# Two heads of a pair issued alternately on the halves of the partitions, in score matmuls and index dots

## The chip, the core and the metric

One core of one Trainium2 chip runs the whole kernel in one launch. TensorE multiplies, VectorE and ScalarE work on the results, GpSimd (POOL) issues some DMAs and small powers, SyncE (SP) issues the loads of the weights. Each has a queue of its own, in program order, and they meet at semaphores. The metric is the device time in microseconds from launch to end. The median of three runs before the change is 2491.6 us.

## What is computed

Two transformer blocks over 256 tokens of width 2048, all in float32. The first block (an attention layer and a retention layer) is not touched. The second has two kinds of attention over 16 heads each, of width 64:

```python
dots = jnp.einsum('bqhd,bsd->bqhs', qi, k_idx).astype(jnp.float32)
index_score = jnp.einsum('bqh,bqhs->bqs', wi.astype(jnp.float32),
                         jax.nn.relu(dots)) * IDX_SCALE
...
_, sel = lax.top_k(index_score, topk)
...
s = jnp.where((dist >= 0)[:, :, None, :], s + bias, NEG_INF)
p = jax.nn.softmax(s, axis=-1).astype(c_sel.dtype)
o_lat = jnp.einsum('bqhk,bqkr->bqhr', p, c_sel)
```

The 16 index heads (width 64) give a score for each pair of query and key, and the 64 best keys of each query are kept. The sliding-window attention (heads of groups 0 and 1 below) has a bias, a window and a sink; the selected attention (groups 2 and 3) has a bias and the selection. Behind both come an output projection and a gated feed-forward layer with a convolution.

## The kernel before

The weights pass in blocks of 16 x 128 rows by 512 columns, each in four chunks. SP loads chunk c of a block into `raw`, ScalarE rounds it to `w_hi` (`round_hi`), VectorE takes the rest, `w_lo` (`split_lo`), and TensorE multiplies: 24 matmuls of 512 columns a chunk (`project`, `output`, with `product`, L364 to L371). `raw`, `w_hi` and `w_lo` have one place per chunk, so the load of chunk c of the next block waits until TensorE is through with chunk c of this one. ScalarE and VectorE run three chunks ahead: `act_blocks` and `vec_blocks` make chunk 3 of this block in slot 0 and chunks 0 to 2 of the next block in slots 1 to 3.

Between the chunks each engine does the attention work that is written for that slot. Its order is fixed by hand, in three lists: `B_STEPS` for TensorE, `B_ACT_STEPS` for ScalarE, and the table in `before` of `vec_second_attention` for VectorE. TensorE's slot c comes behind chunk c. ScalarE's and VectorE's slot c comes ahead of the rounding or the rest of chunk c - 1 of the next block.

Four groups g of eight heads h pass in this way, one during each of the blocks `B_B0 + 5` to `B_B0 + 8`. A head is these steps:

- TensorE, a score step (`s`): two matmuls of keys and queries over 64 partitions. Tokens 0 to 127 see 128 keys, tokens 128 to 255 see 256. Even heads lie in partitions 0 to 63, odd heads in 64 to 127 (`half`), and they write the PSUM banks `sc[0]` and `sc[1]`. The step of head n waits until VectorE has read head n - 2 from its bank (`b_read`).
- VectorE, `head(h)`: adds the bias into `b_s` (this is the read, L2093), in groups 2 and 3 also the selection (L2096), and takes the maxima (L2099; L2103 in groups 0 and 1).
- ScalarE, `s`: two exponentials with their sums (L1829).
- TensorE, `t`: three transposes into `turn` (L1473). ScalarE, `t`: a copy to `b_pT` (L1815).
- TensorE, `v`: three value products into `pair[1]` (L1483 to L1485).

VectorE also looks for the largest index scores in rounds (`topk`) in slots of groups 0 and 1. In group 3, and behind it, it adds each chunk of the output projection to the residual (`vec_scaled_sum`), and TensorE's next chunk waits for the first half of that (`b_scaled`).

The index dots (L1549) come before this, in the block `B_B0 + 3`: after chunks 1, 2 and 3 TensorE does the heads of `INDEX_HEADS`. Each is two matmuls, into `sc[h % 2]`; ScalarE takes the relu (L1767), and VectorE adds it, weighted, to `b_idx` (L2018), one head after the other.

Of the kernel before, what the change touches and what calls it, by code (L numbers as in the profile page):

```python
# [25 lines left out]
P = 128  # L26
D = 2048
T = 256
# [16 lines left out]
COPIES = 32  # L45
VEC_A, VEC_R, VEC_F = 45, 37, 16

INDEX_HEADS = {1: range(0, 4), 2: range(4, 9), 3: range(9, 16)}

A_B0 = 0  # L50
R_B0 = A_B0 + 4 * A_KV
# [64 lines left out]
def build(nc, x, attn_w_in, attn_q_gain, attn_k_gain, attn_w_out, ret_w_in, ret_decay_exp,  # L116
# [5 lines left out]
    with ctx:  # L122
# [90 lines left out]
        b_kBT = take("b_kBT", [8, T])  # L213
# [1096 lines left out]
        def pool_first_block(g):  # L1310
# [113 lines left out]
            with g.Fori(1, R_HEADS - 1) as i:  # L1424
# [5 lines left out]

        B_STEPS = {1: ["s0", "s1", "s2"], 2: ["t0", "s3", "t1", "s4", "v0"],
                   3: ["s5", "t2", "v1", "s6", "t3", "v2", "s7", "t4", "v3", "t5", "v4", "t6", "v5", "t7",
                       "v6", "v7"]}
        B_ACT_STEPS = {1: ["s0", "s1", "s2"], 2: ["t0", "s3", "t1", "s4"],
                       3: ["t2", "s5", "t3", "s6", "t4", "s7", "t5", "t6", "t7"]}
        HALF = W_HD

        def half(h):  # L1440
# [12 lines left out]
        def pe_b_step(pe, g, what):  # L1453
            kind, h = what[0], int(what[1])
            n = 8 * g + h
            if kind == "s":
                pe.wait_ge(sem("b_qT_b"), g + 1)
                pe.wait_ge(sem("b_qT_a"), g + 1)
                if n >= 2:
                    pe.wait_ge(sem("b_read"), n - 1)  # L1460
                keys = (lambda w: b_kaT[half(h), g, 0:w]) if g < 2 else \
                       (lambda w: b_kBT[half(h), 4 * (g - 2) + h // 2, 0:w])
                mm = three(sc[h % 2], lambda to, t, w: pe.matmul(
                    to, b_qT[half(h), h // 2, t * P:(t + 1) * P], keys(w), start=True, stop=True))
                mm.then_inc(sem("b_score"), 1)
            elif kind == "t":
                pe.wait_ge(sem("b_prob"), n + 1)
                if h < 2 and g > 0:
                    pe.wait_ge(sem("b_ol"), 4 if g == 3 else 2 * g)
                if n >= 2:  # L1470
                    pe.wait_ge(sem("b_pT"), n - 1)
                for m in range(3):
                    mm = pe.transpose(turn[h % 2][:, m * P:(m + 1) * P], b_s[:, h % 4, m * P:(m + 1) * P],  # L1473
                                      ident[:, :])
                mm.then_inc(sem("b_p_turned"), 1)
            else:
                pe.wait_ge(sem("b_pT"), n + 1)
                if h == 0 and g > 0:
                    pe.wait_ge(sem("b_og"), g)
                val = (lambda k: b_va[:, k, g * HALF:(g + 1) * HALF]) if g < 2 else \  # L1480
                      (lambda k: b_vB[:, k, (8 * (g - 2) + h) * HALF:(8 * (g - 2) + h + 1) * HALF])
                col = slice(h * HALF, (h + 1) * HALF)
                pe.matmul(pair[1][0][:, col], b_pT[:, h % 2, 0:P], val(0), start=True, stop=True)  # L1483
                pe.matmul(pair[1][1][:, col], b_pT[:, h % 2, P:2 * P], val(0), start=True, stop=False)
                pe.matmul(pair[1][1][:, col], b_pT[:, h % 2, 2 * P:3 * P], val(1), start=False, stop=True)\  # L1485
                    .then_inc(sem("b_pv"), 1)
# [17 lines left out]
        def pe_second_attention(pe):  # L1504
# [31 lines left out]
            def index(c):  # L1536
                if c == 0:
                    pe.wait_ge(sem("i_kdup"), 1)
                    pe.wait_ge(sem("gate_row"), 8)
                    pe_transposes(pe, sc[0], i_kdup, [0]).then_inc(sem("i_k_turned"), 1)  # L1540
                    return
                if c == 1:
                    pe.wait_ge(sem("i_kT"), 1)
                    pe.wait_ge(sem("i_qT_a"), 2)
                    pe.wait_ge(sem("i_qT_v"), 2)
                for h in INDEX_HEADS[c]:
                    if h >= 2:
                        pe.wait_ge(sem("i_relu"), h - 1)
                    three(sc[h % 2], lambda to, t, w: pe.matmul(  # L1549
                        to, i_qT[half(h), h // 2, t * P:(t + 1) * P], i_kT[half(h), 0:w],  # L1550
                        start=True, stop=True)).then_inc(sem("i_dot"), 1)
            project(pe, B_B0 + 3, pair[1], after=index)

# [409 lines left out]
        def vec_second_attention(v):  # L1964
# [110 lines left out]
            for g in range(4):  # L2075
                def start(g=g):
                    if g == 0:
                        v.wait_ge(sem("sink_in"), 16)
                        vec(v.tensor_scalar(b_nsink[:, :], b_sink[:, :], -1.0, None, ALU.mult))
                        topk(2)  # L2080

                def head(h, g=g):

                    n = 8 * g + h
                    if h == 0:
                        v.wait_ge(sem("bias_in"), 16 * 2 * (P // COPIES) * (g + 1))
                        if g == 2:
                            v.wait_ge(sem("sel"), 1)
                    v.wait_ge(sem("b_score"), n + 1)
                    if n >= 4:  # L2090
                        v.wait_ge(sem("b_p_turned"), n - 3)
                    s = b_s[:, h % 4, :]
                    v.tensor_tensor(s, sc[h % 2][:, 0:384], b_bias[:, h, :], ALU.add).then_inc(sem("b_read"), 1)  # L2093
                    v.wait_ge(sem("b_read"), n + 1)
                    if g >= 2:
                        vec(v.tensor_tensor(s, s, b_sel[:, :], ALU.add))  # L2096
                        vec_wait(v)
                    for t, w in ((0, slice(0, P)), (1, slice(P, 384))):
                        ins = v.tensor_reduce(b_nm[:, h, t:t + 1], s[:, w], AX, ALU.max, negate=True)  # L2099
                    if g < 2:  # L2100
                        vec(ins)
                        vec_wait(v)
                        ins = v.tensor_scalar(b_nm[:, h, :], b_nm[:, h, :], b_nsink[:, 8 * g + h:8 * g + h + 1],  # L2103
                                              None, ALU.min)
                    ins.then_inc(sem("b_max"), 1)

                def steps(c, g=g):
                    if g == 0 and c in (1, 2):
                        topk(1)
                    if g == 1 and c == 1:  # L2110
                        topk(1)
                        select()
                def finish(g):

                    if g < 2:
                        v.wait_ge(sem("b_max"), 8 * g + 8)
                        v.tensor_tensor(b_es[:, :, :], b_nm[:, :, :],
                                        b_sink[:, 8 * g:8 * g + 8].unsqueeze(2).to_broadcast([P, 8, NT]),
                                        ALU.add).then_inc(sem("b_esx"), 1)
                        v.wait_ge(sem("b_es"), g + 1)  # L2120
                        vec(v.tensor_tensor(b_ri[:, :, :], b_sum[:, :, :], b_es[:, :, :], ALU.add))
                        vec_wait(v)
                        vec(v.reciprocal(b_ri[:, :, :], b_ri[:, :, :]))
                    else:
                        v.wait_ge(sem("b_prob"), 8 * g + 8)
                        vec(v.reciprocal(b_ri[:, :, :], b_sum[:, :, :]))
                    vec_wait(v)
                    v.wait_ge(sem("b_pv"), 8 * g + 8)
                    if 1 <= g <= 2:
                        v.wait_ge(sem("b_o_turned"), 2 * g)  # L2130
                    if g == 3:
                        v.wait_ge(sem("b_q_turned"), 8)
                    for t in range(NT):
                        ins = v.tensor_tensor(gview(b_out(g)[:, t, :], 8), gview(pair[1][t][:, :], 8),
                                              b_ri[:, :, t].unsqueeze(2).to_broadcast([P, 8, HALF]), ALU.mult)
                    ins.then_inc(sem("b_og"), 1)

                def before(c, g=g):

                    if g == 3:  # L2140
                        vec_scaled_sum(v, "b_scaled", c, CH * (B_B0 + 8) + c + 1, c, pair[0], b_tmp, 0)
                    for h in {1: (0, 1, 2), 2: (3, 4), 3: (5, 6, 7)}.get(c, ()):
                        head(h)
                        if h == 0 and 1 <= g <= 2:
                            vec_b_outT(v, g - 1)
                    if c == 3:
                        finish(g)
                vec_blocks(v, B_B0 + 5 + g, {0: [start], **{c: [lambda c=c, s=steps: s(c)] for c in (1, 2, 3)}}, before)
# [215 lines left out]
```

## Time and profile before

| | |
|---|---|
| time, median of three runs | 2491.6 us (2485.77 to 2497.4) |
| profiled execution, span from the first to the last instruction | 2493.1 us |
| own time of that execution outside the span | not listed; it can't be told which of the three it is |
| granted TensorE clock, mean | 0.957 |
| TensorE (PE) busy | 2324.4 us (93%) |
| weight loads (PEld) busy | 1914.7 us (77%) |
| VectorE (DVE) busy | 1737.8 us (70%) |
| ScalarE (ACT) busy | 962.3 us (39%) |
| index stage (first to last dot) | about 1385 to 1409 us of the span |
| four groups of eight heads | about 1448 to 1638 us of the span |

Busy times overlap. A matmul's record is longer than its share of the stream, since matmuls are pipelined: two records that follow each other overlap by their ends, and the distance from start to start is what a matmul costs. The granted clock is a share of full speed: 1.00 is 2.4 GHz and 0.50 is 1.2 GHz.

### The profile page before, as it was taken

Reading aid. Unit: us, or ns where it says so; the run is one execution under the profiler, and the core shown is the slowest. Engines: PE = TensorE matmul, PEld = TensorE weight load, DVE = VectorE, ACT = ScalarE, POOL = GpSimd, SP = SyncE. Lnnn points to the kernel's source line nnn. Section 1 sums busy time; section 2 is a strip of 40 time slices with the busy share of each in tenths; the row PEclk is TensorE's granted clock in tenths of the full one; section 3 lists DMA queues with packets and bytes.
Section 4 is the critical chain, followed back from the end, with each engine's and each line's share of the span. In section 5 each row is a group of like instructions: output and inputs, shape, how many; then the busy total and the mean of one; then the engine's idle time right before and its main releaser. Section 6 shows DMA issues by size and latency. Waiting matters only on the chain.

```text
span 2493.1 us, 29352 instructions
## 1 busy us (share of the span) xinstructions
PE 2324.4 (93%) x10764; PEld 1914.7 (77%) x10764; DVE 1737.8 (70%) x2035; ACT 962.3 (39%) x987; POOL 178.4 (7%) x194
## 2 busy tenths in 40 slices
PE   6899998779999999999879999998999999999996
PEld 5778887657888888888668777777788888888885
DVE  6787876987877778778773554677466666666666
ACT  3433433333333333333323343434444444444442
POOL 4110000320000000000010000000000000000000
PEclk8999999889999999999988988989999999999998
DMA  6786775458778677787543444334555555555552
GB/s 220 263 267 228 254 257 192 161 202 296 250 245 294 234 261 272 242 274 263 201 137 112 133 123 123 115 119 152 183 188 185 185 185 186 187 188 189 193 185 101
DMA packets 261801, 501.29 MB, mean 201 GB/s; under 512 B 16753, under 2 KB 70289, under 8 KB 261104
## 3 DMA queue, kind: packets, MB, share of 16 engines
q1 hardware_dynamic: 230656, 382.39, 46.5%
q0 software_dynamic: 30512, 114.93, 13.6%
q10 hardware_dynamic: 576, 3.21, 0.3%
q8 instruction: 36, 0.59, 0.1%
q14 instruction: 21, 0.17, 0.0%
HBM read 496.80 MB, written 3.67 MB: 201 GB/s over the span
## 4 chain that ended last, share of the span: by engine, by line
PE 47%; issue 36%; DVE 10%; DMA 4%; ACT 3%; SPq 0%; POOL 0%; DVEq 0%; ACTq 0%; POOLq 0%
PE pair_t L369 13%; PE pair_t L371 13%; PE pair_t L370 13%; DVE m_acc L929 2%; DVE w_lo L363 2%; DMA raw<-in_attn_w_in_dram 2%; ACT w_hi L358 2%; PE sc L688 1%; PE turn L462 1%; PE turn L470 1%; PE sc L680 1%; DVE b_nm L2099 1%; ACT b_s L1829 1%; PE sc L546 1%; DVE b_s L2093 1%
## 5 line engine op out<-in xcount | busy, mean ns | idle before, releaser
L363 DVE TENSOR_TENSOR w_lo<-raw,w_hi 128x2048 fp32r<-128x2048 f32 (+1 forms) x372 | 833.0, 2242 | 546.3 <-ACT w_hi L358 541.2
L358 ACT ACTIVATE w_hi<-raw 128x2048 fp32r<-128x2048 f32 (+1 forms) x372 | 692.8, 1864 | 1147.2 <-DMA raw<-in_ret_w_in_dram 376.2
L369 PE MATMUL pair_t<-w_hi,x_hi 128*128 128x512 f32 (+2 forms) x2112 | 826.8, 391 | 24.1 <-DVE w_lo L363 21.8
L370 PE MATMUL pair_t<-w_lo,x_hi 128*128 128x512 f32 (+2 forms) x2112 | 814.3, 386 | 0.0
L371 PE MATMUL pair_t<-w_hi,x_lo 128*128 128x512 f32 (+2 forms) x2112 | 814.2, 386 | 0.0
L369 PEld LDWEIGHTS pair_t<-w_hi,x_hi 128*128 128x128 f32 x2112 | 404.4, 191 | 106.2 <-issue 18.8
L371 PEld LDWEIGHTS pair_t<-w_hi,x_lo 128*128 128x128 f32 x2112 | 403.5, 191 | 78.9
L370 PEld LDWEIGHTS pair_t<-w_lo,x_hi 128*128 128x128 f32 x2112 | 404.6, 192 | 75.8 <-issue 0.2
L929 DVE SCALAR_TENSOR_TENSOR m_acc<-m_raw,csilu,m_acc 128x512 f32<-128x512 f32 x360 | 278.9, 775 | 15.4 <-DMA m_raw<-in_w_mod_dram 5.1
L369 PE MATMUL pair_t<-w_hi,f_hh 128*128 128x512 f32 x352 | 140.2, 398 | 7.2 <-DVE f_hl L2170 7.2
L371 PE MATMUL pair_t<-w_hi,f_hl 128*128 128x512 f32 x352 | 138.4, 393 | 0.0
L370 PE MATMUL pair_t<-w_lo,f_hh 128*128 128x512 f32 x352 | 137.8, 391 | 0.0
L1340 POOL DMA_DIRECT2D m_raw<-in_w_mod_dram x96 | 73.0, 760 | 857.0 <-DVE m_acc L929 823.9
L369 PE MATMUL pair_t<-w_hi,r_oh 128*128 128x512 f32 x256 | 104.7, 409 | 8.2 <-DVE r_ol L1096 8.2
L370 PE MATMUL pair_t<-w_lo,r_oh 128*128 128x512 f32 x256 | 101.5, 397 | 0.0
L371 PE MATMUL pair_t<-w_hi,r_ol 128*128 128x512 f32 x256 | 101.5, 396 | 0.0
L369 PEld LDWEIGHTS pair_t<-w_hi,f_hh 128*128 128x128 f32 x352 | 66.7, 189 | 21.0 <-DVE f_hl L2170 7.6
L371 PEld LDWEIGHTS pair_t<-w_hi,f_hl 128*128 128x128 f32 x352 | 66.5, 189 | 15.4
L370 PEld LDWEIGHTS pair_t<-w_lo,f_hh 128*128 128x128 f32 x352 | 66.6, 189 | 14.1
L1083 DVE TENSOR_TENSOR z<-z,pair_t 128x512 f32<-128x512 f32 x96 | 61.4, 681 | 15.4 <-PE pair_t L371 15.4
L2281 POOL TENSOR_TENSOR rstd<-var,minus_half 128x2 f32<-128x2 f32 x3 | 2.1, 710 | 901.6 <-DVE var L1929 901.6
L369 PEld LDWEIGHTS pair_t<-w_hi,r_oh 128*128 128x128 f32 x256 | 48.6, 190 | 21.1 <-DVE r_ol L1096 8.4
(323 smaller groups left out, 2185.4 us busy)
## 6 DMA issues: line engine op xcount, KB each, us to landing
m_raw<-in_w_mod_dram POOLq DMA_DIRECT2D x96, 1024.0 KB, 6.9
raw<-in_ret_w_in_dram SPq DMA_DIRECT2D x192, 512.0 KB, 4.5
raw<-in_w_up_dram SPq DMA_DIRECT2D x176, 512.0 KB, 4.2
raw<-in_w_down_dram SPq DMA_DIRECT2D x88, 512.0 KB, 4.5
raw<-in_attn_w_in_dram SPq DMA_DIRECT2D x64, 512.0 KB, 4.6
raw<-in_ret_w_out_dram SPq DMA_DIRECT2D x64, 512.0 KB, 4.7
raw<-in_w_in_dram SPq DMA_DIRECT2D x56, 512.0 KB, 4.6
raw<-in_attn_w_out_dram SPq DMA_DIRECT2D x32, 512.0 KB, 5.7
```

The lines of the kernel that those rows point to most:

```text
L358: act.activation(chunk(w_hi, c, width), chunk(raw, c, width), ACT.Copy).then_inc(sem("hi"), 1)
L363: v.tensor_tensor(chunk(w_lo, c, width), chunk(raw, c, width), chunk(w_hi, c, width).bitcast(F32), ALU.subtract).then_inc(sem("lo"), 1)
L369: pe.matmul(to, xh, wh, start=start, stop=False)
L370: pe.matmul(to, xh, wl, start=False, stop=False)
L371: return pe.matmul(to, xl, wh, start=False, stop=stop)
L462: mm = pe.transpose(to[:, i * P:(i + 1) * P], src[:, t, m * P:(m + 1) * P], ident[:, :])
L470: mm = pe.matmul(turn[0][:, 4 * m + q:4 * m + q + 1], m_acc[:, m, q * P:(q + 1) * P], ones[:, 0:1], start=True, stop=True)
L546: mm = pe.matmul(sc[(h + 1) % 2][:, t * T:(t + 1) * T], a_qT[:, h, t * P:(t + 1) * P], a_kT[:, :], start=True, stop=True)
L680: mm = pe.matmul(sc[0][:, s * T:(s + 1) * T], r_kT[:, k, s * P:(s + 1) * P], r_qT[:, k, :], start=k == 0, stop=k == 1)
L929: ins = v.scalar_tensor_tensor(out=m_acc[:, m, :], in0=w, scalar=cc, in1=m_acc[:, m, :], op0=ALU.mult, op1=ALU.add)
L1083: ins = v.tensor_tensor(z[:, t, c * CB:(c + 1) * CB], z[:, t, c * CB:(c + 1) * CB], pair[order[c]][t][:, :], ALU.add)
L1340: g.dma_start(m_raw[:, c % 2, :, :], w_m[:, CH * c:CH * c + CH, bass.ds((2 * step + m) * CB, CB)])\
```

## The change

The score step takes a pair of heads (`p`), and the index dots go by pairs. Of a pair, the matmul of the even head's first 128 tokens is issued, then the odd head's, then the two of the second 128 tokens. A pair waits for both heads of the pair before (`b_read` at n, `i_relu` at h). Since a step now holds two heads, the lists are written anew: TensorE's score steps stand at p0 (slot 1), p2 (slot 2), p4 and p6 (slot 3), and v0 moves to the start of slot 3. VectorE's heads go from 3, 2, 3 in slots 1, 2, 3 to 2, 2, 4. ScalarE's exponentials go from 3, 2, 3 to 2, 2, 4, by pairs too. The index heads go from 4, 5, 7 to 4, 6, 6.

```diff
-INDEX_HEADS = {1: range(0, 4), 2: range(4, 9), 3: range(9, 16)}
+INDEX_HEADS = {1: range(0, 4), 2: range(4, 10), 3: range(10, 16)}
...
-        B_STEPS = {1: ["s0", "s1", "s2"], 2: ["t0", "s3", "t1", "s4", "v0"],
-                   3: ["s5", "t2", "v1", "s6", "t3", "v2", "s7", "t4", "v3", "t5", "v4", "t6", "v5", "t7",
+        B_STEPS = {1: ["p0"], 2: ["t0", "t1", "p2"],
+                   3: ["v0", "p4", "t2", "v1", "t3", "p6", "v2", "t4", "v3", "t5", "v4", "t6", "v5", "t7",
                        "v6", "v7"]}
-        B_ACT_STEPS = {1: ["s0", "s1", "s2"], 2: ["t0", "s3", "t1", "s4"],
-                       3: ["t2", "s5", "t3", "s6", "t4", "s7", "t5", "t6", "t7"]}
+        B_ACT_STEPS = {1: ["s0", "s1"], 2: ["t0", "t1", "s2", "s3"],
+                       3: ["t2", "t3", "s4", "s5", "t4", "t5", "s6", "s7", "t6", "t7"]}
...
-            if kind == "s":
+            if kind == "p":
                 pe.wait_ge(sem("b_qT_b"), g + 1)
                 pe.wait_ge(sem("b_qT_a"), g + 1)
                 if n >= 2:
-                    pe.wait_ge(sem("b_read"), n - 1)
-                keys = (lambda w: b_kaT[half(h), g, 0:w]) if g < 2 else \
-                       (lambda w: b_kBT[half(h), 4 * (g - 2) + h // 2, 0:w])
-                mm = three(sc[h % 2], lambda to, t, w: pe.matmul(
-                    to, b_qT[half(h), h // 2, t * P:(t + 1) * P], keys(w), start=True, stop=True))
-                mm.then_inc(sem("b_score"), 1)
+                    pe.wait_ge(sem("b_read"), n)
+                keys = (lambda o, w: b_kaT[o, g, 0:w]) if g < 2 else \
+                       (lambda o, w: b_kBT[o, 4 * (g - 2) + h // 2, 0:w])
+                for t, lo, w in ((0, 0, P), (1, P, T)):
+                    for e in range(2):
+                        mm = pe.matmul(sc[e][:, lo:lo + w], b_qT[half(e), h // 2, t * P:(t + 1) * P],
+                                       keys(half(e), w), start=True, stop=True)
+                        if t == 1:
+                            mm.then_inc(sem("b_score"), 1)
...
-                for h in INDEX_HEADS[c]:
+                for h in INDEX_HEADS[c][::2]:
                     if h >= 2:
-                        pe.wait_ge(sem("i_relu"), h - 1)
-                    three(sc[h % 2], lambda to, t, w: pe.matmul(
-                        to, i_qT[half(h), h // 2, t * P:(t + 1) * P], i_kT[half(h), 0:w],
-                        start=True, stop=True)).then_inc(sem("i_dot"), 1)
+                        pe.wait_ge(sem("i_relu"), h)
+                    for t, lo, w in ((0, 0, P), (1, P, T)):
+                        for e in range(2):
+                            mm = pe.matmul(sc[e][:, lo:lo + w], i_qT[half(e), h // 2, t * P:(t + 1) * P],
+                                           i_kT[half(e), 0:w], start=True, stop=True)
+                            if t == 1:
+                                mm.then_inc(sem("i_dot"), 1)
...
-                    for h in {1: (0, 1, 2), 2: (3, 4), 3: (5, 6, 7)}.get(c, ()):
+                    for h in {1: (0, 1), 2: (2, 3), 3: (4, 5, 6, 7)}.get(c, ()):
```

## Rows read from the trace of the kernel before

**Rows 1.** The page's chain that ended last, share of the span by engine.

```profile
PE 47%; issue 36%; DVE 10%; DMA 4%; ACT 3%; SPq 0%; POOL 0%; DVEq 0%; ACTq 0%; POOLq 0%
```

**Rows 2.** Timeline of TensorE, slot 1 of group 0: start, length, line, operation, wait.

```profile
1460.61 0.93 PE L1463 MATMUL sc<-b_kaT,b_qT 64*128 64x128 f32 x8
1462.37 0.89 PE L1463 MATMUL sc<-b_kaT,b_qT 64*128 64x128 f32 x4 [0.83 <-DVE b_s L2093]
1463.19 0.50 PE L369 MATMUL pair_t<-w_hi,x_hi 128*128 128x512 f32 x1
```

**Rows 3.** Chain that ended last, group 0: start, length, what.

```profile
1465.91 0.99 ACT b_s L1829 x4
1466.90 1.81 ACT w_hi L358
1468.74 2.29 DVE w_lo L363
...
1481.72 0.57 DVE b_s L2093
```

**Rows 4.** Timeline of TensorE, end of group 0; its last line, of group 3.

```profile
1482.42 0.89 PE L1463 MATMUL sc<-b_kaT,b_qT 64*128 64x128 f32 x4 [0.72 <-DVE b_s L2093]
1483.24 0.88 PE L1473 MATMUL turn<-ident,b_s 128*128 128x128 f32 x3
1484.63 0.69 PE L1483 MATMUL pair_t<-b_va,b_pT 128*128 128x64 f32 x2 [0.51 <-ACT b_pT L1815]
...
1485.97 0.85 PE L1473 MATMUL turn<-ident,b_s 128*128 128x128 f32 x3
1486.61 0.53 PE L1483 MATMUL pair_t<-b_va,b_pT 128*128 128x64 f32 x2
...
1487.78 0.85 PE L1473 MATMUL turn<-ident,b_s 128*128 128x128 f32 x3
...
1492.65 0.77 PE L369 MATMUL pair_t<-w_hi,x_hi 128*128 128x512 f32 x1
...
1638.22 0.80 PE L369 MATMUL pair_t<-w_hi,b_oh 128*128 128x512 f32 x1 [1.44 <-DVE b_q L2134]
```

**Rows 5.** Windows: tails and next chunks; length, busy PE, PEld, DVE, ACT, POOL; PEclk, DMA, GB/s.

```profile
1482.42:1492.65 10.23, 9.72 (x46) 8.99 (x47) 3.93 (x14) 6.76 (x19) 4.60 (x8) 0.54 0.58 132
1492.65:1500.21 7.56, 7.56 (x26) 6.04 (x26) 5.69 (x4) 2.02 (x2) 0.00 (x0) 0.72 0.15 31
...
1577.90:1585.54 7.64, 6.32 (x48) 5.18 (x47) 3.81 (x10) 5.69 (x18) 4.58 (x8) 1.00 0.54 147
1585.54:1591.13 5.59, 5.59 (x26) 4.54 (x26) 3.49 (x3) 2.86 (x2) 0.05 (x1) 1.00 0.66 139
...
1625.98:1638.22 12.24, 10.06 (x47) 9.06 (x47) 5.92 (x15) 8.43 (x19) 0.00 (x0) 0.53 0.01 1
```

**Rows 6.** Timeline of VectorE: read of head 6, group 0; heads 5 and 6, group 2.

```profile
1483.09 0.55 DVE L2093 TENSOR_TENSOR b_s<-sc,b_bias 128x384 f32<-128x384 f32 x1
...
1576.40 0.55 DVE L2093 TENSOR_TENSOR b_s<-sc,b_bias 128x384 f32<-128x384 f32 x1
...
1578.11 0.55 DVE L2093 TENSOR_TENSOR b_s<-sc,b_bias 128x384 f32<-128x384 f32 x1
```

**Rows 7.** Timeline of TensorE: v3 of group 2.

```profile
1579.64 0.43 PE L1483 MATMUL pair_t<-b_vB,b_pT 128*128 128x64 f32 x2 [0.34 <-ACT b_pT L1815]
```

**Rows 8.** Windows (columns of Rows 5) at a pause of TensorE in the first block.

```profile
404.69:408.10 3.41, 0.00 (x0) 0.00 (x0) 3.38 (x8) 0.00 (x0) 0.00 (x0) 1.00 1.01 380
408.10:418.34 10.24, 7.97 (x22) 6.32 (x23) 4.47 (x7) 2.99 (x3) 2.83 (x4) 0.50 0.45 150
```

**Rows 9.** Timeline of ScalarE: a copy to b_pT in group 0.

```profile
1486.85 0.49 ACT L1815 ACTIVATE b_pT<-turn 128x384 f32<-128x384 f32 x1
```

**Rows 10.** Timeline of TensorE, index dots: heads 2 and 3; heads 13 to 15.

```profile
1386.42 1.30 PE L1549 MATMUL sc<-i_kT,i_qT 64*128 64x128 f32 x8 [0.57 <-ACT i_relu L1767]
...
1405.93 2.62 PE L1549 MATMUL sc<-i_kT,i_qT 64*128 64x128 f32 x12 [0.23 <-ACT i_relu L1767]
```

## The prediction

> **What bounds the kernel now.** I read the page's chain first, then the engine windows over the attention stage, then the timeline of one group of eight heads. TensorE carries the chain with 47% of the span, and 36% is "issue", mostly time inside its own stream [rows 1]. Work taken off TensorE pays only where TensorE, and not something that TensorE waits for, ends last. The changed steps lie in the index stage (about 1385 to 1409 us of the span) and in four groups of eight heads (1448.5 to 1638.2).
>
> In a group TensorE alternates a chunk of projection matmuls with a slot of attention steps. After the first score step of group 0 the chain leaves TensorE: it runs through VectorE's bias add and maxima of heads 0 to 2, ScalarE's exponential of head 2 (0.99), ScalarE's w_hi (1.81), VectorE's w_lo (2.29), and so on, until VectorE reads head 5 at 1481.72 [rows 3]. TensorE's next score step starts at 1482.42, having waited 0.72 for that read, and from there to the next projection at 1492.65 TensorE works through a tail of transposes and value products at half clock (the granted clock is 0.54 over it, which is mostly the 1.2 GHz level) [rows 4, 5]. So a group has two parts: a VectorE and ScalarE part up to the read of head 5, and a TensorE part behind it.
>
> **Part 1, the interleaving itself.** It is meant to let two heads on the two halves of the partitions run side by side. Already now the step with heads 0 and 1, issued one head after the other, takes 0.93 us for 8 records, and the next with head 2 alone takes 0.89 us for 4 [rows 2]. Two heads cost what one costs, in the old order. I cost the interleaving within a pair at nothing (bounds: 0 and -0.1 us a pair, the difference between those rows being 0.04). 
>
> **Part 2, pairs where single heads stood.** Per group the score steps go from one ready pair and six singles to four pairs. On TensorE alone slot 1 ends with the pair, at 1461.5 instead of 1463.19, 1.7 us earlier [rows 2]; slot 2 loses a score step and v0, which goes to slot 3. What decides is whether this passes through the VectorE part. The slots of VectorE go from 3, 2, 3 heads to 2, 2, 4. A head costs VectorE 1.37 us in groups 0 and 1 (from one read's start to the next, 1481.72 to 1483.09 [rows 3, 6]) and 1.71 in groups 2 and 3 (1576.40 to 1578.11) [rows 6]. In slot 1 one head goes, so w_hi, w_lo and all of slot 2 move up by 1.37 (1.71). In slot 3 VectorE starts its heads that much earlier, but it must now do head 4 before head 5. The read of head 5 comes at -1.37 + 1.37 = 0: the same time as now. The last pair (p6) waits for both reads of the pair before, so for head 5, as s7 does now. TensorE arrives at p6 earlier by all that slots 1 and 2 gave, and gives it all back there: it will have done its five earlier steps of slot 3 by about 1477.6 in group 0 (chunk 3 ends near 1474.3, plus some 3.3 for v0, p4, t2, v1, t3) and then wait until about 1482.4, 4.8 us instead of 0.72.
>
> Two costs come behind that. **First, v2 is now queued behind the waiting p6**; now it runs before s7, in time that is free. **Second, the clock.** This trace has a comparable pause of TensorE in the first block: 3.41 us with no matmul, at a granted clock of 1.00, and then 10.24 us at 0.50 [rows 8]. A fall before or during the new pause is thus very likely in each of the four groups, while now group 2 has its whole tail at 1.00 [rows 5].
>
> The tail at half clock, from p6's start:
> - p6: a warm single takes 0.82 (from its start at 1482.42 to the transpose behind it at 1483.24; records overlap at their ends). At half clock the group's tail from v3 on takes 8.02 against 5.90 in warm group 2 (1484.63 to 1492.65; 1579.64 to 1585.54, where the next chunk starts) [rows 4, 5, 7], a factor 1.36; pure streaming would be a factor 2. So 1.1 to 1.6; I take 1.3.
> - v2: 1.17, from transpose to transpose (1485.97 to 1487.78, 1.81) less 0.64 for the transposes (1485.97 to 1486.61). t4: 0.64 [rows 4].
> - from v3 to the end: 8.02, plus a new stall. ScalarE now turns both t4 and t5 before it does exponentials 6 and 7. From v3's start t5 is done at 1.34 + 0.64 = 1.98, its copy takes 0.49 [rows 9], exponential 6 takes 0.99 [rows 3]: about 3.6 with the hand-overs, while TensorE wants t6 at 1.98 + 1.17 = 3.15. That is 0.45 (bounds 0 and 1.3).
> Sum: 1.3 + 1.17 + 0.64 + 8.02 + 0.45 = 11.6 us.
>
> Group 0: 1482.42 + 11.6 = 1494.0 against 1492.65, **+1.4**. Group 1 repeats group 0 (the same steps and forms, 10.2 us of tail as well, half clock in most of it), **+1.4**. Group 2: the read of head 5 starts at 1576.40, as the second of its slot now, and lasts 0.55; p6 at 1577.1, end 1588.7 against 1585.54, +3.2. Then its next projection chunk runs partly cold: 7.56 as behind group 0 instead of 5.59 [rows 5], +2.0; **+5.2**. Group 3: before, 12.24 from 1625.98 [rows 5], with a wait of 1.44 at its end for VectorE's last product [rows 4]; after, 11.6 + 1.4 = 13.0, **+0.8**. In group 3 the scaled sum of each chunk (VectorE) also holds TensorE's chunks, but it moves with VectorE's slots, whose sum is unchanged. Attention: +8.8. Bounds of the unknown terms: p6 -0.2 to +0.3 and stall -0.45 to +0.85 in four groups, so -2.6 to +4.6, and the chunk 0 to +2.
>
> **Part 3, the index stage.** Slot 1 has heads 0 to 3 in both. The second pair now waits for both relus instead of one each; heads 2 and 3 now take 1.30 us together, the second starting some 0.4 late (a single alone takes 0.89), and a common start then, at about 1386.85, ends within 0.1 of it: +0.05. Slot 2 gets a sixth head and slot 3 loses its seventh; in the steady stretch heads follow each other by (2.62 - 0.92) / 2 = 0.85 us, the pace of VectorE's addition [rows 10]: +0.85 and -0.85. I take **+0.2** (bounds -0.5 and +0.9) because the last addition, which the key and value build waits for, may come up to 0.3 later.
>
> No DMA is added or removed. Raw loads are issued after chunks that end earlier by up to 3 us; the load's cover stays, since w_hi follows ScalarE's exponentials and copies rather than a landing. The bias loads behind the last read of a group start where they do now.
>
> **Sum:** +8.8 + 0.2 = +9.0 us on the profiled execution, 2493.1 to 2502.1 of span. That execution's span is 1.5 above the median of the three runs, whose own spread is 11.6; the prediction is 2491.6 + 9.0 = 2500.6 us.
>
> **Rivals.**
> A. *The clock does not fall in the pauses.* p6, v2, t4 then take 0.82 + (1.17 + 0.64) x 5.90 / 8.02 = 2.15, and the rest 5.90: 8.05. Groups 0 and 1: -2.2 each and -2.0 each for the chunk behind; group 2: 1585.15, -0.4; group 3: 8.05 + 1.4 against 12.24, -2.8, and -2.0. Sum -13.6: 2478 us. For it: the clock stood at 1.00 through most of the score slots. Against it: the pause of [rows 8], and that the 0.72 wait was followed by a fall already.
> B. *TensorE is the bound after all*, and what it saves arrives at the end: 1.7 in slot 1 and two single steps of 0.85 a group, 3.4 x 4 = -13.6: again 2478. For it: TensorE has the largest share of the chain [rows 1]. Against it: the chain through groups goes by VectorE and ScalarE until head 5 [rows 3]; it decides only if TensorE reaches p6 after VectorE has read head 5.
> C. *Slower by more.* In place: the projection chunk behind each tail. If the clock comes back only after that chunk, it takes up to 2 x 5.59 = 11.2 us instead of 7.56 [rows 5], 3.6 more in each of four groups: +14.5, with the forecast's 9.0 +23.5, 2515 us, and anything over a fourth of it ends on the slower side of the bound below. It decides from the point where the cold stretch outlasts the tail by a whole chunk. For it: the cold stretch begins with a longer pause than now, and behind the pause of the first block it lasted 10.24 us [rows 8]. Against: the clock returned during the chunk behind group 0 [rows 5].
>
> **Numbers.** Forecast 0.62, A 0.10, B 0.08, C 0.20. The forecast's own range is 2494 to 2507. With A and B cut about in half and most of C the range is 2482 to 2511. 0.5% (12.5 us) is about what a measurement of this kernel can tell from no change. Faster by more: A and B lie just beyond 2479, so somewhat over half of them, 0.10. Slower by more (over 2504): about a fifth of the forecast's weight and nearly all of C, 0.30. Within: 0.60.
>
> **What would show it.** Pair steps of 8 records at 0.9 us; slot 1 followed by its chunk at once; TensorE idle 3 to 5 us before p6, released by VectorE's read; VectorE's read of head 5 within 0.3 us of its distance now from the group's first score; granted clock near 0.5 over all four tails, group 2 included; tails of 11 to 12 us; index stage within 1 us. Wrong if p6 starts without a wait, if the tails show 1.00, or if a step of two heads takes much less than 0.9 us.

## The result, and the profile after

| | before | changed |
|---|---|---|
| median | 2491.54 us (4 runs, 2485.77 to 2497.4) | 2503.51 us (4 runs, 2502.73 to 2503.68) |
| span of the profiled execution | 2493.1 | 2502.0 |
| mean granted clock | 0.957 | 0.956 |

The ratio is 1.0038, with a 95% interval from 1.0026 to 1.0049: slower by 6.5 to 12.2 us, within 0.5%. (The two medians of the table alone are 12.0 us or 1.0048 apart.) The forecast was +9.0 (2500.6). Later runs of the kernel before, on other occasions, had medians of 2494.5 to 2495.4, so part of the 12 us is probably that the first four runs of before were low. The two spans differ by 8.9 us, and the traces say where they lie.

The windows of the changed kernel over the pause ahead of p6 in group 0, its tail and the chunk behind; then the tails of groups 1 and 2, the chunk behind group 2, and the tail of group 3 (columns as in [rows 5]):

```profile
1476.60:1483.83 7.23, 2.17 (x21) 1.62 (x19) 5.54 (x13) 3.78 (x8) 0.00 (x0) 0.85 0.44 145
1483.83:1495.78 11.95, 11.67 (x56) 10.84 (x57) 4.02 (x14) 6.79 (x20) 4.60 (x8) 0.50 0.56 125
1495.78:1502.70 6.92, 6.92 (x27) 5.55 (x27) 5.69 (x4) 2.02 (x2) 0.00 (x0) 0.79 0.06 14
1531.80:1543.75 11.95, 11.67 (x57) 10.84 (x57) 4.02 (x14) 6.79 (x20) 4.61 (x8) 0.50 0.55 129
1580.10:1592.06 11.96, 11.68 (x57) 10.85 (x57) 4.67 (x12) 6.80 (x19) 4.63 (x8) 0.50 0.52 120
1592.06:1598.64 6.58, 6.58 (x26) 5.32 (x26) 3.49 (x3) 1.91 (x2) 0.00 (x0) 0.83 0.12 22
1633.47:1647.10 13.63, 11.92 (x56) 10.89 (x56) 6.01 (x15) 8.47 (x20) 0.00 (x0) 0.50 0.01 1
```

All four tails are at 0.50 from end to end. Before, group 2 had 1.00, groups 0 and 3 had 0.54 and 0.53 [rows 5], and group 1 had 0.59 (1529.31 to 1539.54). In group 0 the granted clock was 0.50 from 1483.3 to 1497.0 before; in the changed kernel it is 0.50 from 1481.6, inside the pause ahead of p6, to 1498.7.

TensorE's timeline shows slot 1 ending with the pair (compare [rows 2]), and p6, v2, t4, v3 and the late t6 in group 0 (compare [rows 4]):

```profile
1462.04 0.93 PE L1465 MATMUL sc<-b_kaT,b_qT 64*128 64x128 f32 x8
1462.89 0.50 PE L369 MATMUL pair_t<-w_hi,x_hi 128*128 128x512 f32 x1
...
1483.83 1.65 PE L1465 MATMUL sc<-b_kaT,b_qT 64*128 64x128 f32 x8 [5.06 <-DVE b_s L2099]
1485.41 0.69 PE L1486 MATMUL pair_t<-b_va,b_pT 128*128 128x64 f32 x2
...
1486.74 0.85 PE L1476 MATMUL turn<-ident,b_s 128*128 128x128 f32 x3
1487.38 0.53 PE L1486 MATMUL pair_t<-b_va,b_pT 128*128 128x64 f32 x2
...
1490.85 0.90 PE L1476 MATMUL turn<-ident,b_s 128*128 128x128 f32 x3 [0.28 <-ACT b_s L1835]
...
1495.78 0.77 PE L369 MATMUL pair_t<-w_hi,x_hi 128*128 128x512 f32 x1
```

The chain of group 0 goes where [rows 3] had it go, with one head less in slot 1 and two heads ahead of the hand-over to TensorE in slot 3:

```profile
1465.96 0.99 ACT b_s L1835 x4
1466.95 1.82 ACT w_hi L358
1468.79 2.29 DVE w_lo L363
...
1481.76 0.57 DVE b_s L2099
...
1483.13 0.56 DVE b_s L2099
1483.69 0.14 issue
1483.83 1.65 PE sc L1465 x8
```

TensorE's waits over 1448 to 1640 for a read of the scores and for the scaled sum (`b_tmp`), first of the kernel before (what waited for what: us in total, times, longest).

```profile
PE sc L1463 <- DVE b_s L2093: 10.0, 7, 3.2
PE pair_t L369 <- DVE b_tmp L1949: 0.5, 1, 0.5
```

The same of the changed kernel. The waits for a read are fewer, longer, and twice as much in sum; those for the scaled sum, all in group 3, go from 0.5 to 5.0 us.

```profile
PE sc L1465 <- DVE b_s L2099: 19.9, 4, 5.1
PE pair_t L369 <- DVE b_tmp L1955: 5.0, 3, 3.9
```

I call the stretch from the start of group 0's first projection chunk to the first chunk behind group 3 the attention stretch. It goes from 189.62 to 197.04 us. From the first index dot to the start of group 0 it is 63.68 before and 63.88 after, +0.20. The first dot itself starts 1.27 later (1384.92, 1386.19), in code that the change does not touch; over all fourteen profiled kernels of this study it starts between 1381.8 and 1386.2. The sum is 1.27 + 0.20 + 7.42 = 8.89 of the 8.9 us.

### The profile page after: what moved, and what is told of

Its sections match the earlier page's. It is cut to its first block, busy times and chain, and to the rows that moved or that the text cites. A ratio compares the mean times of both kernels' runs of the same rounds, so it can differ in the third digit from the quotient of the medians.

```text
span 2502.0 us, 29336 instructions
## 1 busy us (share of the span) xinstructions
PE 2320.3 (93%) x10764; PEld 1917.3 (77%) x10764; DVE 1738.1 (69%) x2035; ACT 961.7 (38%) x987; POOL 177.2 (7%) x194
## 4 chain that ended last, share of the span: by engine, by line
PE 47%; issue 36%; DVE 9%; DMA 3%; ACT 3%; SPq 0%; POOL 0%; DVEq 0%; ACTq 0%; POOLq 0%
PE pair_t L369 13%; PE pair_t L370 13%; PE pair_t L371 13%; DVE m_acc L929 2%; DVE w_lo L363 2%; DMA raw<-in_attn_w_in_dram 2%; ACT w_hi L358 2%; PE sc L688 1%; PE turn L462 1%; PE turn L470 1%; PE sc L680 1%; PE sc L546 1%; DVE b_s L2099 1%; DMA raw<-in_ret_w_in_dram 0%; DMA m_raw<-in_w_mod_dram 0%
```

## Experiments

All were timed beside the kernel before. Group lengths are from the start of a group's first chunk to the start of the next one's (group 3: to the first chunk behind). "Tails at 0.50" names the groups in whose tail the profiled execution had the lower clock, for at least eight tenths of it or ("part of") for less. "Products" in this table are extra matmuls of 128 x 64 whose result is not used. e10 and e12 are the kernel before with products, e9 is e6 with products, and e7, e8 and e11 are the changed kernel with products.

| kernel | median us | ratio to before (95%) | groups 0, 1, 2, 3 | stretch | tails at 0.50 |
|---|---|---|---|---|---|
| before | 2491.5 | | 44.05, 46.89, 46.00, 52.68 | 189.6 | 0, 1, 3 |
| changed | 2503.5 | 1.0038 (1.0026 to 1.0049) | 45.72, 47.97, 48.31, 55.04 | 197.0 | all |
| e1: pairs issued head by head | 2500.35 | 1.0023 (1.0013 to 1.0032) | 45.74, 47.67, 48.15, 54.99 | 196.6 | all |
| e2: v2 ahead of p6 | 2498.22 | 1.0012 (1.0000 to 1.0023) | 44.45, 47.47, 48.07, 54.91 | 194.9 | all |
| e3: single steps, heads 2, 2, 4 | 2500.74 | 1.0026 (1.0016 to 1.0036) | 45.72, 47.85, 48.23, 55.05 | 196.9 | all |
| e4: index part alone | 2493.51 | 0.9999 (0.9989 to 1.0009) | 41.29, 44.90, 47.35, 54.55 | 188.1 | 1, 2, 3 |
| e5: pairs, heads 4, 2, 2 | 2486.95 | 0.9968 (0.9958 to 0.9979) | 41.39, 45.84, 44.96, 51.57 | 183.8 | part of 0, 3 |
| e6: single steps, heads 3, 3, 2 | 2484.61 | 0.9966 (0.9954 to 0.9979) | 42.04, 44.33, 44.14, 49.67 | 180.2 | none |
| e7: changed, pause filled | 2478.27 | 0.9940 (0.9924 to 0.9957) | 41.10, 41.86, 42.45, 49.49 | 174.9 | none |
| e8: v2, then products, then p6 | 2497.10 | 1.0003 (0.9989 to 1.0018) | 46.42, 52.10, 52.17, 51.46 | 202.2 | 0, 1, 2 |
| e9: e6 with products | 2482.18 | 0.9951 (0.9935 to 0.9968) | 40.67, 45.61, 42.67, 50.43 | 179.4 | part of 3 |
| e10: before with products | 2484.84 | 0.9957 (0.9940 to 0.9974) | 41.22, 42.11, 45.52, 54.43 | 183.3 | part of 2, 3 |
| e11: products, then v2, then p6 | 2479.38 | 0.9942 (0.9922 to 0.9962) | 40.44, 41.29, 42.47, 51.89 | 176.1 | 3 |
| e12: before, more products | 2480.36 | 0.9946 (0.9929 to 0.9963) | 41.31, 42.11, 45.42, 52.65 | 181.5 | part of 2 |

**e1, the interleaving undone**

```diff
-                for t, lo, w in ((0, 0, P), (1, P, T)):
-                    for e in range(2):
+                for e in range(2):
+                    for t, lo, w in ((0, 0, P), (1, P, T)):
```

(The same in the index dots.)

> The changed kernel with one thing undone: the matmuls of a pair are issued head by head again, all lists and waits stay. Theory: the alternate issue is worth nothing, since two heads that are ready together already share the time of one. The attention stretch (first projection chunk of group 0 to the first chunk behind group 3; 189.6 us before, 197.0 after) stays at 197.0 within 1, a pair step is 0.93 us for 8 records, the time 2503 within 2. Rival (strict program order makes the old order serial): a pair step takes about 1.6 us, the four last pairs run at half clock, so +5 in attention and +5 in the index stage, about 2513.

The stretch stayed (196.6 against 197.0), and a pair step issued head by head takes what an interleaved one takes. TensorE's timeline of e1, group 0:

```profile
1460.62 0.93 PE L1465 MATMUL sc<-b_kaT,b_qT 64*128 64x128 f32 x8
1461.48 0.50 PE L369 MATMUL pair_t<-w_hi,x_hi 128*128 128x512 f32 x1
```

The alternate issue, the change's first purpose, is worth nothing here. The time, 2500.35, was 3 us below the changed kernel's and missed the 2 us that I had allowed. The two were timed on different occasions, against medians of before that differ by 3.5, and their ratios to before overlap in their intervals.

**e2, v2 ahead of p6**

```diff
-                   3: ["v0", "p4", "t2", "v1", "t3", "p6", "v2", "t4", ...
+                   3: ["v0", "p4", "t2", "v1", "t3", "v2", "p6", "t4", ...
```

> The changed kernel with v2 issued ahead of p6, in the pause, instead of behind it. Theory: v2 sits at the head of the tail and costs its own 1.17 us at half clock in each group, so the stretch goes from 197.0 to 192.3 and the time down by 4.7. The start of p6 against the group's first score step is the same. Rival (the tail is paced by the exponentials of heads 6 and 7, and v2 fills time that is free): no change.

The step was right and its worth was not: -2.1 instead of -4.7. Windows of e2, tail of group 0 and the time behind it:

```profile
1481.68:1492.36 10.68, 10.40 (x51) 9.56 (x51) 4.03 (x14) 6.80 (x20) 4.60 (x8) 0.50 0.50 117
1492.36:1499.80 7.44, 7.44 (x25) 5.97 (x25) 5.69 (x4) 2.01 (x2) 0.00 (x0) 0.69 0.23 46
```

The tail is 1.27 shorter (10.68 against 11.95). The chunk behind takes 7.70 (to the transposes at 1500.06) where the changed kernel's takes 6.92. So 0.78 of the 1.27 went back to the clock: it is at 0.50 for 17.1 us in both kernels (1481.6 to 1498.7, and 1479.9 to 1496.9 in e2), and with a shorter tail more of that lies on the chunk. Group 0 has the full 1.27; groups 1 to 3, each behind such a chunk, have 0.50, 0.24 and 0.13.

**e3, the old single steps in the new distribution**

```diff
-        B_STEPS = {1: ["s0", "s1", "s2"], 2: ["t0", "s3", "t1", "s4", "v0"],
-                   3: ["s5", "t2", "v1", "s6", "t3", "v2", "s7", "t4", ...
+        B_STEPS = {1: ["s0", "s1"], 2: ["t0", "t1", "s2", "s3"],
+                   3: ["v0", "s4", "s5", "t2", "v1", "t3", "s6", "s7", "v2", "t4", ...
```

> The kernel before, with its single score steps and its index stage, but with the heads in slots 1, 2, 3 as 2, 2, 4 on all three engines and v0 and v2 where the changed kernel has them. Theory: the distribution and the order make the cost and not the pair step; s6 moves 1.4 us into the pause, s7 starts when p6 does, the clock falls all the same, and the stretch is 196 to 197. Rival (the wait for both heads of a pair and the longer step are the cost): the stretch comes back to about 189.6 and the time to that of before.

The stretch is 196.9. TensorE's timeline of e3 shows s6 going earlier into the pause (s6 and s7 are the one row of 2.98 us), and the same wait in kind:

```profile
1480.03 2.98 PE L1460 MATMUL sc<-b_kaT,b_qT 64*128 64x128 f32 x8 [3.72 <-DVE b_s L2090]
```

So the pair step and its stronger wait are not the cause either. It is the distribution 2, 2, 4 with its order.

**e4, the index part alone**

> The kernel before with only the index stage changed (pairs, 4, 6, 6 heads). Theory: +0.2 us, within 0.5, from the first dot to the start of group 0; the rest of the measured +12.0 that attention does not hold (+7.4) is not here but in the scatter of the runs of before. Rival: the index stage, or what it does to the stage behind it, holds 3 to 5 us.

63.88 from the first dot to group 0 (before 63.68): +0.20. Over all fourteen kernels this stretch lies on three levels: 63.65 to 63.70 with the old index stage and 63.86 to 63.88 with the new one; 64.10 (e3, old) and 64.16 (e1, new); 65.28 and 65.31 (e6, e10, old) and 65.42 and 65.48 (e11, e5, new). On the first level the clock is at 1.00 throughout; on the others it is at 0.50 for 3.4 us of it, which begin at 1407.3 or 1407.9 on the second and between 1395.0 and 1396.3 on the third. So the index change costs 0.1 to 0.2 us at an equal clock, and two executions on different levels would have shown up to 1.8. The attention steps of e4 are those of the kernel before, and they showed something else. Two windows of e4, over the end of group 0 and inside it:

```profile
1477.57:1488.36 10.79, 8.91 (x67) 7.25 (x65) 7.18 (x22) 6.23 (x20) 4.55 (x8) 1.00 0.53 160
1478.00:1481.40 3.40, 2.66 (x19) 2.16 (x18) 3.29 (x10) 0.15 (x1) 0.00 (x0) 1.00 0.78 290
```

The same steps with the same wait (0.74 us ahead of s7, before: 0.72), and the clock stayed at 1.00: group 0 takes 41.29 instead of 44.05. So before the change the clock of a tail differs from one execution to another with the same attention steps; what decides it, no run here shows. In changed, e1, e2 and e3 it fell in 16 tails of 16.

**e5 and e6, the read of head 5 a slot earlier**

TensorE's list of e5, then that of e6 (the ends are left out; VectorE's and ScalarE's heads move to the same slots):

```diff
+        B_STEPS = {1: ['p0', 'p2'], 2: ['t0', 't1', 'p4', 'v0'], 3: ['t2', 'v1', 't3', 'v2', 'p6', 't4', ...
```

```diff
+        B_STEPS = {1: ['s0', 's1', 's2'], 2: ['t0', 's3', 't1', 's4', 'v0', 's5'], 3: ['t2', 'v1', 's6', ...
```

> The changed kernel with its pairs as p0 p2 in slot 1, p4 in slot 2, p6 in slot 3 (heads 4, 2, 2 on VectorE and ScalarE). Theory: the read that p6 waits for now lies a slot ahead, so p6 runs without a wait, and t4, v3, t5, v4 too. TensorE then waits only for exponential 6, about 2 us, and from there only t6 v5 t7 v6 v7 are left. The stretch (before 189.6, changed 197.0) falls to 176 to 184, depending on whether the clock falls in that wait; the time is 2480 to 2489. Rival (the sum of VectorE's and ScalarE's slots sets the group's end in any distribution): 189 to 197.

> The kernel before, its single steps and its index stage, with one head moved from slot 3 to slot 2: heads 3, 3, 2, s5 at the end of slot 2. Theory: s7 needs the read of head 5, which is now made in slot 2, so TensorE has work through slot 3 without a pause and the clock stays at 1.00; the stretch is 174 to 180, the time about 2478 to 2484, as good as the pairs with 4, 2, 2 or better. If the pairs with 4, 2, 2 are clearly better than this, the pair step has a worth of its own. Rival (distribution doesn't matter): 189.6, the time of before.

Both are faster than both given kernels, e5 inside what was expected, e6 just above its ranges (180.2 and 2484.6). Single steps in 3, 3, 2 do at least as well as pairs in 4, 2, 2, so the pair step shows no worth of its own here either. The waits went to earlier places in the groups, and the clock fell behind them there too (in e5 at 1463.2, in e6 at 1518.4, for 3.4 us each). TensorE's timeline of e5, group 0, p2:

```profile
1462.65 1.13 PE L1462 MATMUL sc<-b_kaT,b_qT 64*128 64x128 f32 x8 [2.20 <-DVE b_s L2096]
```

TensorE's timeline of e6, group 1, s5:

```profile
1516.95 0.89 PE L1460 MATMUL sc<-b_kaT,b_qT 64*128 64x128 f32 x4 [2.30 <-DVE b_s L2090]
```

**e7, the pause filled.** 20 extra products between t3 and p6; they go to columns that v7 overwrites.

```diff
+            elif kind == "f":
+                for _ in range(20):
+                    pe.matmul(pair[1][0][:, 7 * HALF:8 * HALF], ident[:, :], ident[:, 0:HALF],
+                              start=True, stop=True)
```

> The changed kernel with 20 extra small products (128 rows, 64 columns, 0.23 us each, 4.6 us) between t3 and p6, written where v7 writes later; they change no output. Theory: the clock falls because TensorE pauses; with the pause filled the tails run at 1.00, p6 to the next chunk takes 8.3 instead of 11.95, the chunk behind 5.6 instead of 6.9, and the stretch goes from 197.0 to about 180. Rival 1 (the tail is long for another reason than the clock): 197. Rival 2 (such small products do not hold the clock, as they don't bring it back in the tails): 197 to 199, with the granted clock falling all the same.

This tells the clock from all else: p6 starts 21.80 us after the group's first score step, as in the changed kernel (21.79), and the same steps follow. TensorE's timeline of e7, group 0, filler and p6:

```profile
1476.43 4.58 PE L1468 MATMUL pair_t<-ident 128*128 128x64 f32 x40
1481.67 0.93 PE L1462 MATMUL sc<-b_kaT,b_qT 64*128 64x128 f32 x8 [0.66 <-DVE b_s L2100]
```

Windows of e7 over the filler, the tail and the chunk behind:

```profile
1476.43:1481.67 5.24, 4.58 (x42) 4.47 (x41) 5.07 (x13) 1.79 (x6) 0.00 (x0) 1.00 0.33 128
1481.67:1488.91 7.24, 6.41 (x56) 5.85 (x57) 4.03 (x14) 5.74 (x20) 4.09 (x8) 1.00 0.35 87
1488.91:1494.45 5.54, 5.54 (x26) 4.55 (x26) 5.24 (x4) 2.97 (x2) 0.51 (x1) 1.00 0.79 174
```

The tail takes 7.24 instead of 11.95, the chunk 5.54 instead of 6.92. The stretch fell by 22.1 us to 174.9, 5 more than expected, and 80 useless products made the kernel 0.6% faster than before. Of both rivals nothing is left: the clock is what made the tails long, and such products hold it when they fill the pause. The pause ahead of chunk 3 in group 3, 3.91 us for the scaled sum up to 1598.74, was not filled, and behind it the clock was 0.50 from 1599.8 to 1603.2.

**e8, v2 first, then 17 products**

> The changed kernel with v2 ahead of p6 and then 17 extra small products (written where v7 writes later), so that the pause is filled and v2 is out of the tail. Theory: moving v2 gave 2.1 us instead of 4.7 because the tail ran at half clock and each us that it got shorter lengthened the cold part of the chunk behind; at full clock nothing takes it back, so it gives its 0.7 us a group, up to 0.9 where exponential 6 is late: the stretch goes from 174.9 (20 products, v2 behind p6) to 171 to 172. Rival (v2 is hidden behind the exponentials): 174.9.

Missed: the median is 2497.10, where less than e7's 2478.27 was to be expected. The ten runs go from 2487.03 to 2505.54, and the profiled one, with its stretch of 202.2, is the slowest of them, so the size of what it shows is not typical. From here on the products also wait for `b_og`, as v0 does; no trace has TensorE waiting for it. TensorE's timeline of e8, group 1:

```profile
1525.03 0.49 PE L1479 MATMUL turn<-ident,b_s 128*128 128x128 f32 x3
1527.64 0.43 PE L1489 MATMUL pair_t<-b_va,b_pT 128*128 128x64 f32 x2 [2.11 <-ACT b_pT L1824]
1527.91 0.49 PE L1490 MATMUL pair_t<-b_va,b_pT 128*128 128x64 f32 x2
1528.20 0.64 PE L1491 MATMUL pair_t<-b_va,b_pT 128*128 128x64 f32 x2
1528.62 3.62 PE L1470 MATMUL pair_t<-ident 128*128 128x64 f32 x16
```

v2 waits 2.11 us for ScalarE's copy, which is queued behind w_hi and the copies of the queries. Behind that wait the clock falls (at 1528.1, within v2), and the products then run at half clock (the last row has the first 16 of their 34 records) and hold p6 up. In group 0 v2 waits only 0.73 us and the clock falls at 1480.3, 2.0 us into the products; in group 2 it waits 1.68; in group 3 it does not wait, and the tail stays at 1.00. I had put the filler on the wrong side of the wait.

**e9 and e10, products in the other two orders.** `f3` is three products. First e9, then e10, each with parts left out:

```diff
+        B_STEPS = {1: ['s0', 's1', 'f3', 's2'], 2: [... 'v0', 'f5', 's5'], 3: [... 'v4', 'f3', 't6', ...
```

```diff
+        B_STEPS = {1: ['s0', 's1', 'f3', 's2'], ... 3: [... 'v2', 'f3', 's7', 't4', 'f2', 'v3', ...
```

> Single steps with heads 3, 3, 2, and extra small products ahead of s2 (3), s5 (5) and t6 (3). Theory: the stretch of 180.2 contains five cold windows, some 1.7 us each, of which three lie on chunks of groups 1 and 2; without them 173 to 176, the time 2476 to 2481. Rival (these windows lie where VectorE and ScalarE are late anyway): 180.

> The kernel before with extra small products ahead of s2 (3), s7 (3) and v3 (2), nothing else. Theory: part of what the changed kernel lost to the clock is lost before too (its tails in groups 0, 1 and 3 ran at half clock); with the clock held the stretch goes from 189.6 to about 181, the time to about 2486. Then the best filled version shows whether the order of the change is worth anything once the clock is out of the way. Rival (the clock of the tails has another cause than the short waits): 189.

e9 missed: 179.4 instead of 173 to 176, and 2482.18 instead of 2476 to 2481. Groups 0 and 2 held the clock (40.67, 42.67), but group 1 still lost it ahead of s5, where a wait of 1.18 us was left and s5 then ran at half clock:

```profile
1515.29 1.62 PE L1460 MATMUL sc<-b_kaT,b_qT 64*128 64x128 f32 x4 [1.18 <-DVE b_s L2096]
```

e10 is the telling one: the kernel before with its clock held in groups 0 and 1 takes 41.22 and 42.11. Its stretch is 183.3 where 181 was expected, since the clock fell in groups 2 and 3.

**e11 and e12, the best filling of either order.** e11 has 17 products, then v2, then p6, and 15 more behind p2 in group 3. e12 is e10 with the number of products chosen by group.

> The changed kernel with 17 extra small products ahead of v2, both ahead of p6, and 15 more behind p2 in group 3. Theory: v2 ahead of the products made TensorE wait for ScalarE's copy of head 2 with nothing in the queue, and the clock fell in that wait; behind them it finds the copy made. So groups 0, 1 and 2 hold full clock, and lose v2 from the tail: 40.2, 41.0, 41.6 instead of 41.1, 41.9, 42.5 with 20 products; group 3 with the chunk wait filled 49 instead of 49.5; stretch 171 to 172, time about 2475. Rival (v2 is not on the path at full clock): 174.9.

> The kernel before with extra small products ahead of s2, s7 and v3, their number chosen by group (s2: 3, 3, 5, 10; s7: 3, 3, 3, 15; v3: 2, 2, 4, 4). Theory: groups 0 and 1 as in the first filled version of it (41.2, 42.1), group 2 about 42.5 and group 3 about 49 if the clock holds now: the stretch 174 to 177, that is what the filled changed kernel has, and the order of the change is worth nothing beside the clock. Rival (the change's order has a worth of its own, hidden by the clock): this kernel stays 3 us or more above 174.9 with the clock at 1.00.

e11 bears out e8's lesson: products ahead of v2 keep the clock in groups 0 to 2, at 40.44, 41.29 and 42.47 (expected 40.2, 41.0, 41.6). v2 is worth 0.66 and 0.57 in groups 0 and 1 and nothing in group 2. The stretch, 176.1, missed its 171 to 172, most of it in group 3 (51.89 against e7's 49.49 and the 49 expected). There the 15 products did fill the waits for the scaled sum (1.5 us in all, 4.9 in e7) and the clock stayed at 1.00 through chunk 3. But p4 then came 1.6 us sooner behind the start of chunk 3 (6.32, in e7 7.93), p6 had to wait 1.84 instead of 0.25, and the clock fell 1.0 us behind its start. TensorE's timeline of e11, group 3:

```profile
1613.65 0.93 PE L1462 MATMUL sc<-b_kBT,b_qT 64*128 64x128 f32 x8 [1.84 <-DVE b_s L2102]
```

e12 missed its stretch (181.5), because the clock fell in group 2 all the same, with waits of 0.33 and 0.48 for ScalarE left in the tail:

```profile
1566.57 0.43 PE L1486 MATMUL pair_t<-b_vB,b_pT 128*128 128x64 f32 x2 [0.33 <-ACT b_pT L1818]
1568.27 0.43 PE L1486 MATMUL pair_t<-b_vB,b_pT 128*128 128x64 f32 x2 [0.48 <-ACT b_pT L1818]
```

Where both orders hold the clock, in groups 0 and 1, before's takes 41.31 and 42.11 and the change's 41.10 and 41.86 (e7). The change's order is then worth 0.2 us a group. In group 2 that stays open, since no filled version of before's order held the clock there. In group 3 e12 had 1.00 from 1579.0 to 1626.8; from its second chunk to its end (1583.66 to 1627.02) it took 43.36, and e7 took 42.35 (1580.36 to 1622.71, with 3.4 us of it at 0.50). So the change's order was worth at least 1.0 us there, with other numbers of products in the two, so that part is not separated. No version was shown to be better than e7; e11 and e12 are within its interval.

## Why the prediction was right

**The interleaving at nothing.** Right, by e1. The Trainium skill ("TensorE: Matmul & The Clock Gate", Part 3) states that matmuls keep strict program order in start and end, and that a weight load overlaps a running matmul only where the row groups differ; that row groups overlap only as neighbours is read out of these two. By that reading e1 was expected to be about 10 us slower. Its stretch did not move, and in its trace the last matmul of each head, the one that raises the semaphore, starts within 14 ns of the other's (1461.161 and 1461.175), although the other matmuls of the second head stand between them in program order. The measurement decides against the rule for fp32 matmuls on two row halves.

**The read of head 5 comes at the same time as now, and TensorE gives all its gain back in a pause.** Right. From the group's first score step to the start of that read it is 21.11 us before (1460.61 to 1481.72) and 21.09 after (1462.04 to 1483.13). In groups 1, 2 and 3 it is 21.09, 21.53 and 26.89 before and 21.08, 21.51 and 26.88 after. The pause was forecast at 4.8 and is 5.06, 5.01, 4.93 and 4.87 us in the four groups. e3 shows that the distribution makes it, and not the pairs. Rival B would have needed TensorE to reach p6 after VectorE had read head 5; it was there about 5 us too early in every group. In group 3 part of what TensorE gained went into another pause, 3.92 us ahead of chunk 3 for the scaled sum (1618.55), where before its longest wait for that was 0.51; the forecast names the scaled sum but has no such pause.

**The clock falls in the pause.** Right, and shown by e7: without the pause the same steps run at 1.00. In group 0 it fell at 1481.6, 2.8 us into the pause. Rival A priced a clock that stays at -13.6 us; e7, which forces it, has -14.7 against the stretch of before (with a tail of 7.24 where A had 8.05). Its size was about right and its condition never held.

**The tail at half clock.** 11.6 forecast, 11.95 measured. p6 takes 1.58 (1483.83 to 1485.41), and I had 1.3, between the factor 1.36 of the mixed tail and the 2 of pure streaming. For scores it is 1.84 (the same step takes 0.86 at full clock, 1481.67 to 1482.53 in e7). The new stall behind t5 is there, 0.28 instead of 0.45. v2 and t4 are 1.33 and 0.64 (I had 1.17 and 0.64).

**By groups**, change of a group's length, forecast and measured: group 0, +1.4 and +1.67; group 1, +1.4 and +1.08; group 2, +3.2 and +2.31; group 3 with the chunk behind group 2, +2.8 (0.8 + 2.0) and +2.36. Sum +8.8 and +7.42. The term that was mis-sized most is the chunk behind a tail. I left those behind groups 0 and 1 as they were and took 7.56 for the one behind group 2; they took 6.92 (before 7.56), 6.82 (1543.75 to the transposes at 1550.57; before 8.02, 1539.54 to 1547.56) and 6.58. That is 0.64, 1.2 and 1.0 less than in my sum, 2.8 in all. The tails erred the other way: 0.35 us too short in groups 0 to 2 (p6 and v2) and 0.6 in group 3 (13.63 for 13.0). So more than half of the chunks' error was hidden, which was luck. A longer cold tail leaves less of the cold stretch for the chunk, and e2 shows the same exchange from the other side. Rival C, which had the chunk become longer, was wrong for this reason.

**The index stage.** +0.2 forecast and measured in changed and e4, and the other kernels at an equal clock have 0.1 to 0.2 (see e4). How it comes about, the longer last addition that the forecast assumed, no run shows.

**What was not in the sum:** 1.27 us ahead of all changed code, the scatter of the upstream part. It stood in for the 1.4 us by which attention fell short, so that 8.9 of span met 9.0 by luck. Nor did the sum hold that before's own time differs with the clock from one execution to another (e4). I had read that one execution's half-clock tails as a property of the kernel. The forecast came out close in part because that execution was a typical one; against e4's group 0 the same tail would have been forecast at +4.2.

## What to carry to other kernels

When steps are redistributed between slots, follow the engine that feeds the waits and not the one that is relieved: a read needed by the last step stays where it is if as much work is put ahead of it as was taken away, and the relieved engine only waits longer. Here one long pause of TensorE was worse than several short ones, since it cost the clock of all that followed in the group; price a pause by the rows behind it at the lower level. Move the wait to where projection work stands behind it (e5, e6), or fill it, with the filler ahead of every wait and not behind it (e7, e8, e11). And look at the granted clock of the same stretches before two profiles are compared: it alone made 2.8 us between two executions of one group's steps (before and e4).

## What the runs showed of the hardware that was not expected

- Useless matmuls pay. 20 products of 128 x 64 in each of four pauses, 4.6 us each, took 22.1 us off the stretch. They held the clock at 1.00 where they filled the pause (e7); behind a wait of 0.73 us they did not (e8, group 0). Products and transposes of the same sizes did not bring it back either: in all tails of the changed kernel it stayed at 0.50, in groups 0 and 1 for 11.95 us with TensorE busy for 11.67 of them. It came back 2.9 us into the projection chunk behind group 0 in the changed kernel and 4.6 us into it in e2.
- At half clock a score step takes 1.58 instead of 0.86, a group of three value products 1.17 to 1.33 instead of 0.71, three transposes 0.64 instead of 0.33 to 0.39.
- Two heads' fp32 matmuls on the two halves of the partitions share their time in whichever order they are issued: 0.93 us for 8 records (before, changed, e1), where one head alone takes 0.92 for 4 (index dot at 1396.34 before).
- A wait of 0.72 or 0.74 us ahead of the same step was followed by a fall of the clock in one execution and not in another (before and e4). The 16 tails of changed, e1, e2 and e3 all ran at 0.50; ahead of p6 (in e3 ahead of s6) they have waits of 2.0 to 5.1 us.
